# Second block's attention: the compressed branch in one unit a pair, the convolution and pool mixers on GpSimd, row tiles in the order 3, 0, 2, 1

## What is computed

```python
def hybrid_layer(x, norm_w, w_in, w_out, conv_w, pe_cmp, w_cmp_k, w_cmp_v, pool_w, pool_scale):
    h = rmsnorm_2(x, norm_w)
    p = split_cols(h @ w_in)
    o_a = dsa_mixer(...)         # attention over the keys that an index score chose
    o_b = nsa_mixer(...)         # g0 * compressed + g1 * chosen blocks + g2 * window
    o_c = shortconv_mixer(p['c_b'], p['c_c'], p['c_x'], conv_w)
    o_d = pool_mixer(p['d_u'], pool_w, pool_scale)
    mixed = jnp.concatenate([jax.nn.silu(p['a_gate']) * o_a, jax.nn.silu(p['b_gate']) * o_b,
                             jax.nn.silu(p['c_gate']) * o_c, jax.nn.silu(p['d_gate']) * o_d], axis=-1)
    return x + mixed @ w_out
```

## Time and profile before

| | |
|---|---|
| median of 3 runs | 2786.03 us (2779.63 to 2788.52) |
| profiled execution, its own time | 2785.77 us |
| its span | 2784.0 us |
| TensorE busy | 2618.0 us (94%) |
| GpSimd busy | 1865.3 us (67%) |
| VectorE busy | 1100.4 us (40%) |
| ScalarE busy | 779.9 us (28%) |
| mean granted TensorE clock | 0.974 of full speed |

### The profile page before, as it was taken

One profiled execution on the slowest core, in us unless ns is written; L12 is line 12 of the kernel. 1 busy time (PEld: TensorE's weight loads), 2 busy tenths in 40 slices (PEclk: granted clock), 3 DMA queues, 4 the chain that ended last, 5 costly groups with the idle time before them and its releaser, 6 DMA issues. The chain is left out here.

```text
span 2784.0 us, 35997 instructions
## 1 busy us (share of the span) xinstructions
PE 2618.0 (94%) x13720; PEld 2115.1 (76%) x13724; DVE 1100.4 (40%) x1836; ACT 779.9 (28%) x1587; POOL 1865.3 (67%) x1554
## 2 busy tenths in 40 slices
PE   5998899999999999998899999999998997989797
PEld 4887677877878887887667877888887974788656
DVE  3544773111220112444674111210112498526983
ACT  4342474100120112242474000120111234314161
POOL 4646704888898888746803888898886871367504
PEclk9999999999999999999999999999999997999889
DMA  4322201333333334322201333333333330143202
GB/s 133 97 62 68 61 1 43 91 94 92 106 91 97 96 95 114 98 65 65 69 1 38 88 95 91 91 95 99 95 98 91 93 85 20 38 90 90 69 1 76
DMA packets 159259, 214.51 MB, mean 77 GB/s; under 512 B 51696, under 2 KB 69360, under 8 KB 159088
## 3 DMA queue, kind: packets, MB, share of 16 engines
q1 hardware_dynamic: 120336, 207.27, 25.9%
q10 hardware_dynamic: 38752, 4.95, 1.3%
HBM read 210.06 MB, written 2.10 MB: 76 GB/s over the span
## 5 line engine op out<-in xcount | busy, mean ns | idle before, releaser
L370 POOL TENSOR_TENSOR weight_parts<-weight_ring,zero 128x512 fp32r<-128x512 f32 (+4 forms) x730 | 789.2, 1081 | 765.5 <-PE ps L459 371.5
L373 POOL TENSOR_TENSOR weight_parts<-weight_ring,weight_parts 128x512 fp32r<-128x512 f32 (+3 forms) x804 | 1059.0, 1317 | 136.0 <-ACT weight_parts L381 77.8
L461 PE MATMUL ps<-h_feature_major_high,weight_parts 128*128 128x512 f32 x2304 | 589.2, 394 | 9.7 <-POOL weight_parts L370 9.4
L461 PEld LDWEIGHTS ps<-h_feature_major_high,weight_parts 128*128 128x128 f32 x2304 | 428.5, 188 | 116.2 <-POOL weight_parts L370 16.8
L459 PE MATMUL ps<-weight_parts,h_feature_major_high 128*128 128x512 f32 (+3 forms) x1904 | 430.9, 364 | 20.5 <-POOL weight_parts L370 7.8
L459 PEld LDWEIGHTS ps<-weight_parts,h_feature_major_high 128*128 128x128 f32 x1904 | 334.9, 190 | 73.1 <-POOL weight_parts L370 11.2
L461 PE MATMUL ps<-h_feature_major_low,weight_parts 128*128 128x512 f32 x1152 | 309.6, 391 | 0.0
L459 PE MATMUL ps<-weight_parts,ut_high 128*128 128x512 f32 x1008 | 251.5, 390 | 1.1 <-POOL weight_parts L370 0.9
L461 PEld LDWEIGHTS ps<-h_feature_major_low,weight_parts 128*128 128x128 f32 x1152 | 217.0, 188 | 46.0
L459 PE MATMUL ps<-weight_parts,h_feature_major_low 128*128 128x512 f32 (+3 forms) x952 | 227.9, 361 | 0.0
L459 PEld LDWEIGHTS ps<-weight_parts,ut_high 128*128 128x128 f32 x1008 | 188.3, 188 | 43.6 <-POOL weight_parts L373 2.2
(11 more groups left out here) (284 smaller groups left out, 2985.6 us busy)
## 6 DMA issues: line engine op xcount, KB each, us to landing
weight_ring<-in_w_in SPq DMA_DIRECT2D x272, 256.0 KB, 2.6
weight_ring<-in_w_mlp SPq DMA_DIRECT2D x256, 256.0 KB, 2.6
weight_ring<-in_w_out SPq DMA_DIRECT2D x64, 256.0 KB, 2.6
weight_ring<-in_w_mem_kv SPq DMA_DIRECT2D x32, 256.0 KB, 2.7
weight_ring<-in_w_diff_o SPq DMA_DIRECT2D x32, 256.0 KB, 2.6
weight_ring<-in_w_in SPq DMA_DIRECT2D x32, 170.0 KB, 2.3
weight_ring<-in_w_in SPq DMA_DIRECT2D x32, 168.0 KB, 2.2
weight_ring<-in_w_in SPq DMA_DIRECT2D x32, 163.0 KB, 2.2
```

Of the source, the lines that this page charges most:

```text
L370: self.nc.gpsimd.tensor_tensor(high, raw, self.m["zero"][:].broadcast_to([P, raw.shape[1]]), ALU.add).then_inc(self.s["slab_high"], 1)
L373: self.nc.gpsimd.tensor_tensor(low, raw, high.bitcast(F32), ALU.subtract).then_inc(self.s["slab_split"], 1)
L461: last = self.nc.tensor.matmul(banks[:, t, :], w[:, cut], h, **ends)
```

## The change

In the table of units, each pair now begins with one unit for the compressed branch of all four row tiles: four products of 128 queries with 31 keys side by side in a bank, one maximum, one exponential without bias, and one scaling over 128 x 2 x 4 x 31 (functions `scores_by_tile`, `shift_by_tile`, `scale_by_tile`, `turn_by_tile`, `weight_by_tile`), instead of four units. The causal units of a pair follow in the order of row tiles 3, 0, 2, 1. This leaves 9 units a pair for the NSA mixer instead of 12, and 26 in all. The last 4 of the 16 rounds of the choice for the last row tile move between units (`LATER`). The convolution, the pool mixer's arithmetic and the split of the convolution's result move from VectorE to GpSimd, between the splits of the second and third slab of `wo0`; since GpSimd gets the convolution's second and third tap as a product and a sum, it has some more instructions. ScalarE takes one exponential of a single column ahead of the units.

```diff
-                between[name]()
+            if between and (name, k) in between:
+                between[name, k]()
...
+    def shift_by_tile(self, u):
+        dve.wait_ge(self.s["scores"], u + 1)
+        src = self.m["ps"][:, 2 * (u % 2):2 * (u % 2) + 2, 0:32 * a["tiles"]].rearrange("p j (t n) -> p j t n", n=32)[:, :, :, 0:a["width"]]
+        out = a["stats"][:, 0]
+        v.tensor_reduce(out, src, AX.X, ALU.max, negate=True)
+        v.drain()
+        v.tensor_scalar(out, out, 1e20, None, ALU.min)
+        v.drain()
+        v.tensor_tensor(self.by_tile(u), src, bc(out, [P, 2, a["tiles"], a["width"]], 3), ALU.add).then_inc(self.s["maxed"], 1)
...
+        units.append(dict(shared, kind=0, i=0, n=TT * NCMP, tiles=TT, width=NCMP, mask=(m["cmp16"], 0), last=False,
+        for i in (3, 0, 2, 1):
...
-            L.split_slabs(pool)
+            def causal_mixers():
+                L.emptied(pool, "f2")
+                pool.wait_ge(s["index_added"], TT - 1)
+                g.tensor_tensor(u[:, :, 16:], fm[:, 6:8, :], fm[:, 8:10, :], ALU.mult)
+                g.tensor_tensor(fm[:, 10:12, :], fm[:, 10:12, :], fm[:, 4:6, :], ALU.mult)
+                g.drain()
...
+                g.drain().then_inc(s["pooled"], 1)
+
+            L.split_slabs(pool, {("wo0", PARTS): causal_mixers})
...
+            a.activation(m["warm"][:], m["zero"][:], ACT.Exp)
             A.steps(0, U, (3, A.copy), (0, A.exp))
...
-            choose(3)
+            last_rounds = choose(3, LATER)
...
-            A.steps(0, U, (0, A.maximum), (1, A.scale), (4, close), between={2 + k: lambda k=k: piece(k) for k in range(len(ops))})
+            A.steps(0, U, (0, A.maximum), (1, A.scale), (4, close), between={2 + 2 * k: r for k, r in enumerate(last_rounds)})
```

More of the change, by code:

```diff
@@ L624, in steps, with by_tile, scores_by_tile @@
                 between[i]()
+    def by_tile(self, u):
+        a = self.units[u]
+        return self.m["probs"][:, u % 3, :, 0:32 * a["tiles"]].rearrange("p j (t n) -> p j t n", n=32)[:, :, :, 0:a["width"]]
+    def scores_by_tile(self, u):
+        pe, a, last = self.nc.tensor, self.units[u], None
+        out = [self.m["ps"][:, 2 * (u % 2) + j, 0:32 * a["tiles"]].rearrange("p (t n) -> p t n", n=32)[:, :, 0:a["width"]] for j in range(2)]
+        for j in range(2):
+            pe.matmul(out[j], self.m["ident16"][:], a["mask"][0][:], start=True, stop=False)
+        for t in range(a["tiles"]):
+            for j in range(2):
+                last = pe.matmul(out[j][:, t, :], a["q"][j][:, t * P:(t + 1) * P], a["k"][j], start=False, stop=t == a["tiles"] - 1)
+        last.then_inc(self.s["scores"], 1)
@@ new lines, in scale_by_tile @@
+    def scale_by_tile(self, u):
+        dve, v, a = self.nc.vector, self.nc.vector, self.units[u]
+        dve.wait_ge(self.s["exped"], u + 1)
+        r, p_ = a["stats"][:, 1], self.by_tile(u)
+        v.tensor_reduce(r, p_, AX.X, ALU.add)
+        v.drain()
+        v.tensor_scalar(r, r, 1e-30, None, ALU.max)
+        v.drain()
+        v.reciprocal(r, r)
+        v.drain()
+        v.tensor_tensor(r, r, a["gate"], ALU.mult)
+        v.drain()
+        v.tensor_tensor(p_, p_, bc(r, [P, 2, a["tiles"], a["width"]], 3), ALU.mult).then_inc(self.s["scaled"], 1)
@@ new lines, in turn_by_tile @@
+    def turn_by_tile(self, u):
+        pe, a, last = self.nc.tensor, self.units[u], None
+        pe.wait_ge(self.s["scaled"], a["scaled"])
+        if u >= 1:
+            pe.wait_ge(self.s["turned_copied"], u)
+        p_ = self.by_tile(u)
+        for j in range(2):
+            for t in range(a["tiles"]):
+                last = pe.matmul(self.m["ps"][0:a["width"], 4 + j, t * P:(t + 1) * P], p_[:, j, t, :], self.m["ident"][:], start=True, stop=True)
+        last.then_inc(self.s["turned"], 1)
@@ L627, in scores, with weight_by_tile @@
+    def weight_by_tile(self, u):
+        pe, a, last = self.nc.tensor, self.units[u], None
+        pe.wait_ge(self.s["turned_copied"], u + 1)
+        for j in range(2):
+            last = pe.matmul(self.m["ps"][64 * j:64 * (j + 1), a["bank"], 0:a["tiles"] * P], a["v"][j],
+                             self.m["probs_t"][0:a["width"], u % 2, j, 0:a["tiles"] * P], start=True, stop=False)
+        last.then_inc(self.s["weighted"], 1)
     def scores(self, u):
@@ L708, in scale @@
             return
+        if "tiles" in a:
+            self.scale_by_tile(u)
+            return
         dve.wait_ge(self.s["exped"], u + 1)
@@ L739, in maximum @@
                                  AX.X, ALU.max, negate=True)
-        if a.get("may_be_empty"):
-            dve.drain()
-            last = dve.tensor_scalar(out, out, 1e20, None, ALU.min)
         last.then_inc(self.s["maxed"], 1)
@@ L763, in copy @@
         rows, width = min(P, a["n"]), max(P, a["n"])
+        if "tiles" in a:
+            rows, width = a["width"], P * a["tiles"]
         if "joined" in a:
@@ L1879, in choose, with take @@
                 v.drain()
-                for _ in range(TOPK // 8):
+                def take():
                     v.max(top8, work[:, 0:n])
@@ L1884, in choose, with close_choice @@
                     v.drain()
-                v.tensor_scalar(chosen[:, i, 0:n], work[:, 0:n], MARK, NEG, ALU.not_equal, ALU.mult).then_inc(s["chosen"], 1)
+                def close_choice():
+                    take()
+                    v.tensor_scalar(chosen[:, i, 0:n], work[:, 0:n], MARK, NEG, ALU.not_equal, ALU.mult).then_inc(s["chosen"], 1)
+                rounds = [take] * (TOPK // 8 - 1) + [close_choice]
+                for r in rounds[:len(rounds) - later]:
+                    r()
+                return rounds[len(rounds) - later:]
             choose(1)
```

125 lines of the change are left out of this document (69 added, 56 removed).

## The result

The changed kernel takes 2773.51 us (median of six runs, 2771.32 to 2773.88), the kernel before 2786.97 in the same comparison (six runs, 2779.63 to 2792.09): a ratio of 0.9948, interval 0.9937 to 0.996. It is 13 us faster, where 2795 us was forecast. The profiled execution has a span of 2772.1 us, at a mean granted clock of 0.98.

The account below looks back on a forecast made before the run. VectorE, and TensorE at half clock, were taken to carry the attention stage. 2785.77 us plus 4 for later stage ends and 5 for the clock gave 2795 us; own range 2784 to 2812 (0.62), wider range 2752 to 2812.

Parts of the forecast that it names:

- the end of pair 0: Last scalings of layer 0's first pair: VectorE and GpSimd run in turn, ending at 2357 to 2359 us; before, 2352.25.
- GpSimd's chain: Moved mixer operations on GpSimd: 37 to 41 us of work from 2307.3 us; with turns and drains, ending near 2355.
- (a): Stage's start: convolution and four rounds leave VectorE's head, cutting TensorE's 14.5 us wait to 2 us.
- (b): Compressed branch, eight units become two: TensorE saves 0.9 us a pair, VectorE 3 us a pair by estimate.
- (c): Attention stage without GpSimd's effect: pair 0 at pair 1's pace, some 78 us instead of 96.1 and 98.7.
- rival 4: The reordering or the single unit does nothing by itself; inside the sum, at 1 to 2 us; no chance given.
- Row order at nothing: Row tiles in order 3, 0, 2, 1: at most a microsecond of waits, counted at nothing.
- The "45 us" behind pair 0: Rest of the stage after pair 0's last scalings: 45 us, where 48.5 us follow in the kernel before.
- Clock: Sparse TensorE work in the stage lowers its granted clock: 2.5 us a layer, together +5 us.
- Rival 1: Attention stage: no standstill that counts, moved work costs VectorE nothing; stage 78 us, whole kernel 2747 us; chance 0.12.
- Rival 2: Attention units: half a standstill, one wait a unit instead of two, clock stays up; 2766 us (2755 to 2782); chance 0.18.
- Rival 3: Pair 0: TensorE's gaps keep it at 1.2 GHz, 10 us a layer, 2810 us; 0.08 for worse than 2812, with longer chain.

Follow-up runs that it names:

- without mixers: Changed kernel with the arithmetic of convolution and pool mixer left out on GpSimd, so those outputs are not computed: 2736.54 us.
- the fill: Eight unread score products of 512 columns put into TensorE's pause: 2787.72 us on the kernel before, 2773.40 us on that with the single unit alone.
- cut instructions: Changed kernel with the mixers' 1024-wide GpSimd instructions cut in two, four, eight or sixteen: 2760.4, 2754.5, 2740.0 and 2760.1 us.
- eighths: Changed kernel with each 1024-wide instruction of the mixers on GpSimd cut in eight of 128: 2739.95 us, 0.9827 of before.
- rows in order: Changed kernel with its row tiles in the order 0, 1, 2, 3 again, as in the kernel before: 2777.74 us, ratio 0.9959.

## Why the prediction was wrong, step by step

The step that failed is the end of pair 0: the prediction let GpSimd's chain wait 22 times for VectorE and then added the last scalings. That put the end of pair 0 at 53.4 us from the stage's start, and it came at 46.5 and 49.1. The steps in order:

**(a) The head.** The wait of 14.5 us went, to 1.54 us (the prediction left 2). The timeline of TensorE in the changed kernel:

```profile
2308.87 2.08 PE L701 MATMUL ps<-arena 64*128 64x512 f32 x4 [1.54 <-ACT probs L822]
```

But it was nobody's loss: the kernel with the unit alone keeps the wait and is as fast (2772.85 us). In pair 0 VectorE sets the pace, and it is busy in TensorE's pause.

**(b) The unit: mis-sized.** The prediction read VectorE's saving nearly right (3 us a pair by estimate; 3.6 measured) and then put only TensorE's 0.9 us a pair into the sum. VectorE's saving stood in step (c) alone, as what VectorE would need at full pace. The unit by itself moves the run by 16.3 us (2789.18 to 2772.85 in its own comparison), of which 12.5 us are in the two stages; the rest isn't separated. So rival 4, the single unit at 1 to 2 us, is refuted. It is not what made the sum wrong, though: the sum takes the end of pair 0 from GpSimd's chain, which already counts with the single unit, and behind pair 0 the stages take 46.2 and 44.4 us where 45 stood.

**(c) Pace without standstill.** 77 to 78 us was forecast; without mixers the stage takes 72.6 and 72.3 us. Row order at nothing: confirmed.

**GpSimd's chain: two terms failed, one each way.** Its own time was 37 to 41 us; the operations add up to 41.8. Most of the two-input ones of 1024 take 2.35 us, as worked out (2.39). A scalar product of 512 takes 1.56 to 1.82 us, where 0.6 to 1.04 stood; six of them are 10 us, not 3.6 to 6.2. Against that, the 22 turns of 0.3 us that GpSimd was to give to VectorE don't exist: the chain runs from 2307.50 to 2350.94, 43.4 us, which is its operations and the drains (42.3 us in layer 1), where 47.2 us was forecast. VectorE waits for GpSimd, not the other way.

**The end of pair 0: the step that failed.** "Then the last scalings of the pair, some 3 us more: 2357 to 2359" was 2351.35, 0.4 us behind the chain. So the rhythm was right in layer 0, the two engines do run in turn and end together, but 22 turns (6.6 us) and most of a remainder of 3 us were added that the trace doesn't have; the scalar products at 10 us, not 3.6 to 6.2, took some of that back. Scalar products leave VectorE nearly free for 10 of the 43 us (2312.59 to 2319.63 and 2322.32 to 2325.42), in which it catches up. In layer 1 the turns are missing too, but the remainder is there: the chain ends at 2663.44 and the last scaling of pair 0 at 2667.59, 4.2 us behind it. The "45 us" behind pair 0 are 46.2 and 44.4. Of the marks that the prediction named, the scalings ending with GpSimd's operations is right, "1 to 3 us each" is 0.5 to 4.6 for a pair of scalings, and the chain ends at 2350.9 for "near 2355".

**Clock.** +2.5 us a layer, with "under 0.8 from 2310 to 2355" as its mark. The mark holds, at 0.77, but the kernel before had 0.62 there, and in pair 0 VectorE doesn't wait for TensorE. What the clock costs lies behind pair 0, where VectorE does wait, for 7.7 us in layer 0. Five microseconds there, in the changed kernel (columns as in the earlier trace rows):

```profile
2355.00:2360.00 5.00, 5.00 (x30) 3.63 (x28) 2.98 (x11) 2.71 (x8) 0.00 (x0) 0.53 0.00 0
```

The five before them are at 0.50. Behind pair 0 the clock is 0.91 in layer 0 and 0.97 in layer 1, against 1.00 in both layers without mixers, where that part takes 43.8 us. By that difference the term is at most 2.4 us in layer 0 and 0.6 in layer 1, an estimate: right in size in the first, too high in the second. The premise, that gaps lower the clock and density raises it, isn't borne out by the fill: 0.50 stands behind a filled pause, and in the kernel with the unit alone the stretch 2320 to 2345 is at 0.83 behind an unfilled one.

**The sum.** Forecast: stages of 101.6 and 102.2 us. Measured 92.7 and 93.5, together 17.6 us less, of which 11 us are at the end of pair 0; with the 3.6 us at the border, which no term foresaw, it makes the 21 us between 2795 and 2773.5.

**Rivals.** Rival 1 (no standstill) is refuted by every run with cut instructions. Rival 2 (half a standstill, 2766 us, own range 2755 to 2782) has the measured time in it, by luck. Its mechanism is not what happens: there isn't one wait a unit instead of two, but whole waits beside two-input operations and short ones beside scalar products. Rival 3 (the clock, 10 us a layer) didn't occur. The sign was lost at the end of pair 0, with 6.9 and 4.3 us too many where the whole forecast was +9. That the move is harmful was right (+5 us alone, +3 us with the rest). What outweighs it is the unit, which gives 16 us alone, and which the prediction held to be worth 1 to 2.

The Trainium skill (SBUF — State Buffer, Who interferes with whom) says that who issues first has the shared ports for the whole instruction and the other blocks fully. For two-input operations on GpSimd the cut instructions agree (1.69 us of wait at 2.35 us, 0.22 at 0.48). For GpSimd's scalar products the trace differs: 3 us long, they cost a scaling 0.33 us in the mean. Its other sentence that was weighed, about 6 us for a first call after a load of code (GPSIMD Engine Reference, 2.1 Instruction dispatch), shows nowhere: GpSimd is idle for 0.24 us ahead of its first scalar product in layer 0.

## What to carry to other kernels

Before work is moved to GpSimd beside VectorE, list VectorE's operations in that stretch and ask for each what it would wait for; if the stretch is VectorE's, the moved work comes back as waiting, and here more came back than had been moved away (2.2 and 3.1 us a stage more). Cut GpSimd's two-input instructions as short as its chain has room for, since the wait goes with the length of one instruction and the chain's own end often has slack. And price each part of a change on the engine that sets the pace: the pause of an engine that doesn't is no gain, and four small units made one were worth more than all the rest of the change.

## What the runs showed of the hardware

**GpSimd's times by width.** Two-input float32 operations take about 2.35 us for 1024 columns (1.89 to 2.01 for two sums of a buffer with itself, shifted), about 1.27 for 512, 0.73 for 256, 0.48 for 128 and 0.29 for 64, so a cut to eighths makes the same work 1.6 times as long. A product by a scalar (512 columns 1.56 to 1.82 us, 1024 columns 2.85 to 3.06) is slower than a two-input operation, and the gentler neighbour.

**VectorE beside GpSimd's two-input operations.** Not held up: reductions, maximum and replacement, reciprocals, and the two-input operation of line 655, which has one input in PSUM (0.42 us with and without). Held up: scalings, small products (128x2) and small scalar operations (128x8: 1.85 us at 2344.60 for 0.17 alone), two-input operations with both inputs in SBUF. GpSimd's COPY holds VectorE too: the scalings from 2328.07 end at 2331.78, 0.21 us behind the copy's end.

**The border of the layers.** The time between the stages is 220.6 to 224.5 us, whatever was changed. It goes with the granted clock after TensorE's gap there, here from 2447 to 2475 us in the kernel before and in the changed one:

```profile
2447.00:2475.00 28.00, 20.50 (x106) 20.23 (x106) 8.60 (x16) 9.98 (x18) 9.86 (x12) 0.76 0.58 98
```

```profile
2447.00:2475.00 28.00, 23.58 (x150) 23.41 (x151) 7.18 (x12) 8.23 (x11) 14.29 (x18) 0.94 0.61 112
```

The changed kernel is 3.2 us ahead there. Over the same code, the 20 us that begin 60 us behind the pool matmuls, the clock is 0.84 and 1.00.

The changed kernel and the one with eighths have the short border, the one with rows in order has the long one (0.76), though no code differs there. So up to 4 us of a comparison of two kernels can lie in a stretch that neither touches. Read the stages, not only the span. What decides between the two was not found.
